# Two of the adaLN modulation rows computed in another stage: 64 slabs of the modulation weights taken out of the sequence stage of a hybrid SSD/Hyena/MoE layer and summed on VectorE and GpSimd in the branch stage

## The reference

```python
def adaln(cvec, w, b, n):
    m = jax.nn.silu(cvec) @ w[:, :n * D_MODEL] + b[:n * D_MODEL]
    return jnp.split(m[..., None, :], n, axis=-1)      # sh1, sc1, gt1, sh2, sc2, gt2

h0f, h0b = context_states(...)                # end states of the context, both directions
out_x, _, _ = mixer(hx @ w_in[i], rows, h0f, h0b, lp)
x = x + gt1 * out_x                                    # gate of the mixer: row 2
x = x + gt2 * hier_moe(modulate(rmsnorm(x, norm2_g[i]), sh2, sc2), *moe_args)   # rows 3, 4, 5
```

## Time and profile before

| what | value |
|---|---|
| median of 3 runs | 2380.22 us (2379.96 to 2381.55) |
| the profiled execution's own time | 2379.28 us |
| its span, first to last instruction | 2377.7 us |
| mean granted TensorE clock | 0.970 |
| busy: PE, DVE, ACT, POOL | 93%, 64%, 44%, 4% of the span |
| sequence stage | 402 to 606 us |
| branch stage, slabs 0 to 67 | 614 to 809 us |
| DMA | 500.56 MB, mean 211 GB/s |

### The profile page before, as it was taken

One profiled execution on the slowest core, in us unless ns is written; L12 is line 12 of the kernel. 1 busy time (PEld: TensorE's weight loads), 2 busy tenths in 40 slices (PEclk: granted clock), 3 DMA queues, 4 the chain that ended last, 5 costly groups with the idle time before them and its releaser, 6 DMA issues. The chain is left out here.

```text
span 2377.7 us, 31493 instructions
## 1 busy us (share of the span) xinstructions
PE 2205.3 (93%) x11874; PEld 1752.8 (74%) x11874; DVE 1521.5 (64%) x2066; ACT 1044.4 (44%) x1347; POOL 104.3 (4%) x119
## 2 busy tenths in 40 slices
PE   5779998899899999999999999997899999999995
PEld 0268887445689977777778999986688888778784
DVE  1254556556465467878775454554677777899897
ACT  2333333111455433333333343442655555677774
POOL 1000000000000011111201100000000000000000
PEclk9989999999999999999999999998999999999997
DMA  9923233999757654344433465662478888899993
GB/s 361 358 81 95 83 98 103 348 335 331 229 168 239 178 162 137 111 129 120 150 120 107 131 184 169 217 200 69 135 268 264 289 279 264 308 360 387 359 355 140
DMA packets 301461, 500.56 MB, mean 211 GB/s; under 512 B 18757, under 2 KB 158624, under 8 KB 299926
## 3 DMA queue, kind: packets, MB, share of 16 engines
q1 hardware_dynamic: 296694, 481.54, 60.7%
q0 software_dynamic: 4640, 17.30, 2.1%
HBM read 496.65 MB, written 2.13 MB: 210 GB/s over the span
## 5 line engine op out<-in xcount | busy, mean ns | idle before, releaser
L187 DVE TENSOR_TENSOR w_lo<-raw,w_hi 128x1024 fp32r<-128x1024 f32 x720 | 875.4, 1238 | 516.6 <-ACT w_hi L183 498.9
L183 ACT ACTIVATE w_hi<-raw 128x1024 fp32r<-128x1024 f32 x720 | 751.6, 1058 | 724.1 <-PE bank L195 549.9
L193 PE MATMUL bank<-h,w_hi 128*128 128x256 f32 (+1 forms) x896 | 294.1, 328 | 28.8 <-DVE w_lo L187 28.8
L194 PE MATMUL bank<-h,w_hi 128*128 128x256 f32 (+1 forms) x896 | 290.9, 325 | 0.0
L195 PE MATMUL bank<-h,w_lo 128*128 128x256 f32 (+1 forms) x896 | 290.9, 325 | 0.0
L1327 PE MATMUL bank<-h,w_hi 128*128 128x512 f32 x768 | 275.2, 402 | 0.0
L1329 PE MATMUL bank<-h,w_lo 128*128 128x256 f32 x768 | 215.8, 281 | 0.0
L193 PEld LDWEIGHTS bank<-h,w_hi 128*128 128x128 f32 x896 | 173.8, 194 | 42.8 <-issue 25.8
L195 PEld LDWEIGHTS bank<-h,w_lo 128*128 128x128 f32 x896 | 173.6, 194 | 13.0
L194 PEld LDWEIGHTS bank<-h,w_hi 128*128 128x128 f32 x896 | 173.7, 194 | 12.9 <-issue 0.5
L1327 PEld LDWEIGHTS bank<-h,w_hi 128*128 128x128 f32 x768 | 144.8, 189 | 37.5 <-issue 3.7
(11 more groups left out here) (425 smaller groups left out, 3622.4 us busy)
## 6 DMA issues: line engine op xcount, KB each, us to landing
raw<-in_w_in SPq DMA_DIRECT2D x240, 512.0 KB, 4.1
raw<-in_ada_w SPq DMA_DIRECT2D x192, 512.0 KB, 8.1
raw<-in_moe_w_gate SPq DMA_DIRECT2D x128, 512.0 KB, 5.1
raw<-in_moe_w_up SPq DMA_DIRECT2D x128, 512.0 KB, 5.7
raw<-in_moe_w_down SPq DMA_DIRECT2D x128, 512.0 KB, 6.1
raw<-in_w_ssd_out SPq DMA_DIRECT2D x32, 512.0 KB, 4.5
raw<-in_w_hy_out SPq DMA_DIRECT2D x32, 512.0 KB, 3.5
raw<-in_w_o SPq DMA_DIRECT2D x32, 512.0 KB, 4.6
```

Source lines behind the costliest of these rows:

```text
L183: act.activation(self.k.w_hi[:, j % HL, :], self.k.raw[:, j % RAW, :], ACT.Copy).then_inc(self.hi_ready, 1)
L187: dve.tensor_tensor(self.k.w_lo[:, j % HL, :], self.k.raw[:, j % RAW, :], self.k.w_hi[:, j % HL, :].bitcast(F32), ALU.subtract).then_inc(s ...
L193: pe.matmul(out, lhs[0], rhs[0], start=start, stop=False)
L194: pe.matmul(out, lhs[0], rhs[1], start=False, stop=False)
```

## The change

The rows 2 and 5 (gt1 and gt2) are no longer computed in the sequence stage. Its loop has still four rounds, and a round now computes half of row 3 or of row 4: 16 slabs, one for each tile of 128 rows, by `ada_half`. `ada_quarters` multiplies a slab by four matmuls of 256 columns, into four strips; a part is two slabs in place of four. ACT, POOL and the DMAs of the row handle 256 columns of each strip in place of 512.

The 64 slabs of rows 2 and 5 are loaded in the branch stage, one behind each of the weight slabs 0 to 63, on the same SP queue, into a ring `mring` of three slabs. Even slabs (row 2) are for DVE: behind every second split, from the fifth on, `gate_step` adds slab times silu(c) of the tile's 128 rows (one value per partition) to `msum`, one instruction over 1024 columns with two inputs in SBUF. Odd slabs (row 5) are for POOL: a multiplication in place by silu(c), spread over 1024 columns, then an addition to its half of `msum`, each with two inputs in SBUF. SP waits, before it issues the slab n, for the sum with slab n-3. The bias is loaded into `msum` before the first sum. What is left, the sum over the 128 partitions, is done by PE after slab 83 (`gate_totals`, eight matmuls with ones); ACT copies the result and POOL writes the rows 2 and 5 to `ada_rows`. Two semaphores are dropped elsewhere (`pool_turn`, and `ready`, whose place `h2` takes).

```diff
+        def ada_half(i, j):
+            return ada_w[:, j:j + 1, ds(i * SUB + 3 * D, SUB)]
+        def ada_gate(m):
+            h, kt = m // 2 // KT, m // 2 % KT
+            c0 = (2, 5)[m % 2] * D + h * SUB
+            return ada_w[:, kt:kt + 1, c0:c0 + SUB]
+        def ada_quarters(pe, bank, kt, w):
+            for n in range(4):
+                mm = pe.matmul(bank[32 * n:32 * n + 32, 0:256], k.cpad[:, kt, :], w[:, 0, n * 256:(n + 1) * 256],
+                               start=(kt == 0), stop=(kt == KT - 1))
+            return mm
...
-                st.feed(sp, GROUPS, 32, lambda i, j: ada_src(i + 2, j), s.ada_used, lambda j: z_src(0, j))
+                st.feed(sp, GROUPS, KT, ada_half, s.ada_used, lambda j: z_src(0, j))
...
-                        for j in range(4 * part, 4 * part + 4):
-                            st.wait_full(pe, g, 32, j)
-                            ada_strips(pe, k.psum[0], j, st.slot(j, 1)).then_inc(s.ada_used, 1)
+                        for j in range(2 * part, 2 * part + 2):
+                            st.wait_full(pe, g, KT, j)
+                            ada_quarters(pe, k.psum[0], j, st.slot(j, 1)).then_inc(s.ada_used, 1)
...
-                st.feed(sp, 1, 192, branch_src, st.lo_ready, lambda j: hyo_src(0, j))
+                for n in range(192):
+                    sp.wait_ge(st.lo_ready, n + 1 + st.base)
+                    st.load(sp, n, branch_src(0, n + RAW) if n + RAW < 192 else hyo_src(0, n + RAW - 192))
+                    if n < MODS:
+                        if n >= 3:
+                            if n % 2:
+                                sp.wait_ge(s.mod_dve, (n - 3) // 2 + 1)
+                            else:
+                                sp.wait_ge(s.pool, (n - 3) // 2 * 2 + 3)
+                        sp.dma_start(mring[:, n % 3:n % 3 + 1, :], ada_gate(n)).then_inc(s.mod_full[n % 3], 16)
 
             @block.gpsimd
             def _(pool):
+                pool.memset(msum[:], 0.0).then_inc(s.pool, 1)
...
+                def gate_steps(first, last):
+                    for m in range(first, last):
+                        rows = msum[:, 4 + 2 * (m // KT):6 + 2 * (m // KT), :].rearrange("p a n -> p (a n)")
+                        slab = mring[:, (2 * m + 1) % 3, :]
+                        pool.wait_ge(s.mod_full[(2 * m + 1) % 3], 16 * ((2 * m + 1) // 3 + 1))
+                        pool.tensor_tensor(slab, slab, k.cpad[:, m % KT, 0:1].to_broadcast([P, SUB]),
+                                           ALU.mult).then_inc(s.pool, 1)
+                        pool.wait_ge(s.pool, 2 * m + 2)
+                        pool.tensor_tensor(rows, rows, slab, ALU.add).then_inc(s.pool, 1)
+                gate_steps(0, 20)
                 pool.wait_ge(z.lo, GROUPS)
...
+                gate_steps(20, MODS // 2)
...
+                def gate_totals():
+                    pe.wait_ge(z.kept, 7)
+                    pe.wait_ge(s.mod_dve, MODS // 2)
+                    pe.wait_ge(s.pool, MODS + 1)
+                    for c in range(8):
+                        n = 32 * (c % 4)
+                        mm = pe.matmul(k.psum[6 + c // 4][n:n + 32, :], k.ones[:, 0:32], msum[:, c, :], start=True, stop=True)
+                    mm.then_inc(z.turned, 1)
...
+                def gate_step(m):
+                    rows = msum[:, 2 * (m // KT):2 * (m // KT) + 2, :].rearrange("p a n -> p (a n)")
+                    dve.wait_ge(s.mod_full[2 * m % 3], 16 * (2 * m // 3 + 1))
...
+                    dve.scalar_tensor_tensor(out=rows, in0=mring[:, 2 * m % 3, :], scalar=k.cpad[:, m % KT, 0:1], in1=rows,
+                                             op0=ALU.mult, op1=ALU.add).then_inc(s.mod_dve, 1)
                 for n in range(HY0):
                     st.split_lo(dve, 0, 192, n)
+                    if n >= 4 and n % 2 == 0 and n - 4 < MODS:
+                        gate_step((n - 4) // 2)
```

More of the change, by code:

```diff
@@ L1099, in _ @@
                     own.leave(GROUPS)
-        st.done += 128
+        st.done += 64
         k.ys_hi = place("ys_hi", [P, KT, L], F32R, at=free)
@@ L1171, in build @@
         ktab = place("p6_ktab", [P, 4, 512], at=after("p6_hs"))
+        mring = place("mod_ring", [P, 3, SUB], at=k.where["p6_x2"][0])
+        msum = place("mod_sum", [P, 8, 512], at=k.where["p6_hs"][0])
+        mrows = place("mod_rows", [P, 2, 512], at=k.where["p6_hs"][0])
+        assert after("mod_ring") <= k.where["p6_hs"][0] and after("mod_sum") <= after("p6_ktab")
+        MODS = 4 * KT
         s = Box()
+        s.mod_dve, = sems("p5", "mod_dve")
+        s.mod_full = sems("p5", "mod_full0", "mod_full1", "mod_full2")
         (s.zeroed, s.tables, s.w3, s.decay, s.padded, s.summed, s.conved, s.folded, s.turned,
@@ L1235, in _ @@
                 pool.dma_start(idft[:], consts["idft"]).then_inc(s.tables, 16)
+                gate_steps(20, MODS // 2)
+                pool.wait_ge(s.pool, MODS + 1)
+                pool.wait_ge(s.mod_dve, MODS // 2)
+                load_filter(0)
+                pool.wait_ge(z.kept, 8)
+                for a, c0 in ((0, 0), (1, 3 * D)):
+                    pool.dma_start(ada_rows[:, c0:c0 + D].rearrange("a (n c) -> (a n) c", n=4), mrows[0:P:32, a, :]
+                                   ).then_inc(s.tables, 16)
                 for i in range(5):
@@ L1310, in _ @@
                 pe.wait_ge(z.sig, 1)
-                pe.wait_ge(s.tables, 48)
+                pe.wait_ge(s.tables, 32 + 48)
                 def project(b):
@@ L1397, in _ @@
                         project(6 * i + pp)
+                        if i == 0 and pp == 3:
+                            gate_totals()
                         if i and pp == 0:
@@ L1529, in _ @@
                         st.split_hi(act, 0, 192, HY0 + 4 * b + 3)
+                        if i == 0 and pp == 4:
+                            act.wait_ge(z.turned, GROUPS + 1)
+                            for a in range(2):
+                                ins = act.activation(mrows[:, a, :], k.psum[6 + a][:], ACT.Copy)
+                            ins.then_inc(z.kept, 1)
                         if i and pp == 1:
@@ L1649, in decayed @@
                         dve.wait_ge(s.vmm, n)
+                    else:
+                        dve.wait_ge(s.tables, 32 + 48 + 32)
                     for m in range(4):
@@ L1816, in build @@
             "spread", "added", "lhi", "gfold", "gs", "hsm")
[L1817 removed]
+        s.stored, = sems("p12", "stored")
         w_gate = io["moe_w_gate"][0].rearrange("e (kt p) f -> p e kt f", p=P)
@@ L1898, in _ @@
                 for t in range(TT):
-                    sp.wait_ge(s.ready, t + 1)
+                    sp.wait_ge(s.h2, TT + t + 1)
                     sp.dma_start(io["out"][0, t * P:(t + 1) * P, :], k.x[:, t, :]).then_inc(s.stored, 16)
```

31 lines of the change are left out of this document (18 added, 13 removed).

## The result

| | before | changed |
|---|---|---|
| median | 2380.09 us (2379.72 to 2381.55, 4 runs) | 2436.32 us (2432.66 to 2438.27, 4 runs) |
| span of the profiled execution | 2377.7 us | 2436.7 us |
| mean granted TensorE clock | 0.970 | 0.956 |
| first split of the branch stage | 612.6 us | 600.8 us |
| first product of the Hyena projection (behind slab 67) | 810.8 us | 865.9 us |

The changed kernel is slower: ratio 1.0233, 95% interval 1.0216 to 1.0251. The forecast was 2431. The three marks split the 59.0 us between the spans: the sequence stage gave back 11.8, the branch stage up to slab 67 cost 265.1 - 198.2 = 66.9, and all behind it 3.9. The prediction had -31, +80 and +2. The last of the three is the weakest: the same stretch takes 1563 to 1577 us in the profiled executions of the experiments, though the edits hardly touch it.

A forecast was written before the change was run, and what follows sets the result against it. It took a chain through several engines to bound the sequence stage and PE, 2.87 us a weight slab, the branch stage. 2379.3 - 31 + 80 + 2 = 2430, and 0.9 for the median: 2431 us; 8-in-10 range 2384 to 2466.

The forecast's parts named there:

- -31: Sequence stage: four rounds with fewer slabs give back 9.1 + 9.1 + 6.1 + 7 us; bounds 26 to 36.
- +80: Branch stage: DVE and POOL exclude each other, slab 67 ends at 889 instead of 809 us; bounds 37 to 108.
- +2: After the slabs: `gate_totals` adds eight matmuls over four strips, 8 x 0.24 = 2 us of PE.
- the spread product: POOL's multiplication in the branch stage: taken at 2.40 us like L1227, bounded below by the memset's 0.95 us.
- a product of another time than L1227's: Branch stage, sign of a wrong prediction: POOL's product takes a time other than L1227's 2.40 us.
- become PE idle time, worth nothing: Sequence stage: slabs removed ahead of the third `within`, which waits for DVE, leave PE idle and gain 0 us.
- the 2.4 us that `ada(7)` was to give: Sequence stage, behind the third `within`: `ada(7)` takes 1.0 us instead of 3.4, giving 2.4 us in a round.
- keep their distance: Sequence stage: pieces from the carried products to the third `within` keep their spacing, all starting 6.7 us earlier.
- A: Rival, branch stage: exclusion doesn't bite, POOL's work falls into DVE's idle time and sums are hidden; 2351 us, 11 in 100.
- B: Rival, branch stage: no exclusion, but the DMA engines' bound costs 16 us; 2367 us, 4 in 100.
- C: Rival, branch stage: POOL's spread product is cheap, so the cost is 37 instead of 80 us; 2388 us, 10 in 100.
- D: Rival, branch stage: the slower pace lets TensorE's clock fall, 40 us more; 2471 us, 10 in 100.

The follow-up runs named there:

- e2: Changed kernel without POOL's product and sum on the gate slabs, all 64 slabs still loaded and DVE's sums kept: 2371.77 us, ratio 0.9974 to the kernel before.
- e3: Changed kernel with POOL's product and sum replaced by memsets that only write, of 1024, 2048 and 2048 columns: 2379.03 us, ratio 0.9999 to the kernel before.
- e5: Changed kernel plus 16 unused 128 x 128 matmuls ahead of each round's third `within`: 2428.61 us, ratio 1.0203 to the kernel before.
- e6: Changed kernel plus 16 dummy matmuls ahead of the third `within` and 8 ahead of the carried products: 2423.72 us, ratio 1.0188 to the kernel before.
- e8: Changed kernel with row 5 back in the sequence stage, only row 2 summed in the branch stage, by DVE: 2370.63 us, ratio 0.9970 to the kernel before.
- e1: Changed kernel with the 64 gate slabs neither loaded nor summed, the sequence stage's part alone: 2370.55 us, ratio 0.9966 to the kernel before.

## Why the prediction came out right

**What bounds the branch stage: shown.** POOL's reads and DVE's two-input instructions exclude each other: e2 (no POOL work) and e3 (as much POOL work, no reads) both give the splits back their 1.22 us. The rows that carried it, three blocked instructions in a trace where the two engines met rarely, were enough.

**+80, measured +67.** The mechanism was right, one term too large: the spread product, for which no row stood. I gave it the 2.40 us of L1227 and it takes 1.89. A pair is then 3 x 1.08 + 1.8 + 2.3 = 7.3 us, which is what the timeline shows, in place of 7.84. Thirty-two pairs are 235 us, the eight held up beside them 9; POOL's part runs from 611.0 to 858.6 + 3.3 = 861.9, 251 us (260 predicted), and 7 us are not accounted for. It begins 10.2 us behind the first split (8.4 predicted), and PE is at the Hyena projection 4 us behind its end (8 predicted). The prediction had named a product of another time than L1227's as a sign of being wrong, and it came: right was the mutual exclusion, wrong the price of one of its terms.

**-31, measured -12.** This step failed: the slabs that go "become PE idle time, worth nothing", and the 2.4 us that `ada(7)` was to give behind it. That the pieces up to the third `within` "keep their distance" held where the clock did not interfere: 21.73 us from the carried products to it in the earlier trace rows and in the changed kernel's third round. The idle time cost something. The wait ahead of the third `within` grew from 1.36 to 3.63 us as it had to, and behind it TensorE's granted clock is 0.51 to 0.54 in all four rounds, nearly the 1.2 GHz level: 1.36 + 0.87 + 1.68 us in the third round's three pieces (540.75, 544.04, 545.91), 3.6 to 4.1 us in a round, 15 in four. A round gave 2.9 us instead of 9.1. e5 shows the cause: the wait filled with work that nobody needs, 11.6 us come back, and 13.2 in e6 (10.6 and 13.6 counted from the stage's first product). The rest, 5 to 8 us, I put down to the slow pace at the starts of the rounds: in the third round the first slabs take 3.64 us in place of 1.93 and the states 4.29 in place of 3.70. With these 2.3 us and the 3.9 the predicted round of 42.0 us becomes 48.2, and the third lasts 48.1. Which wait makes the starts slow is read from the rows and was not tested.

The sign was in the earlier trace rows. The prediction took `ada(7)` at 3.4 us beside its own 1.92 for four undisturbed slabs and booked the 2.4 us as slabs saved; 1.5 of them were the half pace behind the wait of 1.36 us, at the very place where the change was to lengthen the wait. The bounds of this term were too narrow also by their own rule: four times the smallest round is 4 x 6.1 = 24.4, not 26, and the 12 measured lie far outside.

**+2, measured +4.** Within what two profiled executions can tell.

**The rivals.** A (no exclusion) fell by the splits of 2059 ns. B (DMA) fell by e2. C had the direction right, the spread product is cheaper, but at 1.89 us it is nearer to L1227 than to the memset's 0.95. D (the clock falls in the branch stage) did not decide: the granted clock is 0.95 and 0.92 there, and PE waits for DVE, which is busy 85.1 of 88 us. The clock acted in the sequence stage, where I had used it only for a bound.

That the total came out 5.3 us off (2436.3 against 2431) is luck: two terms were too large by 19 and 13 us, with opposite signs, and the third added 2.

## What to carry to other kernels

Before work goes to POOL because it is idle, look for a place where POOL reads SBUF beside DVE's two-input instructions, and add the durations of both instead of taking the longer; if DVE has room for the work alone, that is the cheaper place. Idle time on PE is not always free: read the durations and the granted clock of the pieces behind the wait, in the kernel before too, and try dummy matmuls in it. Move work only as far as the chain in the old stage gives time back: three rows in the sequence stage with the fourth row's sums on DVE (e8, ratio 0.9970) cost nothing that these runs can tell against two rows and no sums at all (e1, 0.9966).

## What was not expected of the hardware

Behind a wait of 2.61 us the pieces of e8 take 1.71 and 2.56 us in place of 1.07 and 2.00. Behind one of 1.36 us, in the kernel before, the pace halves in two of four rounds (3.47 us in place of 1.92 in the earlier trace rows) and not at all in the other two. VectorE's one-input multiplication L1633 took 1255 ns beside POOL instructions that only write, 483 without them. A DMA share of 1.05 at 376 GB/s left PE busy in 99.4 of 100 us (e2).
